# One-hot rows of 16 tokens in four instructions, and matches of ranks in half precision, in a two-block transformer kernel

## The chip, the core and the metric

The kernel runs on one NeuronCore of a Trainium2 chip. The metric is the device time of one execution in microseconds (us), the median over several executions.

## The reference, cut to what matters

The reference is two blocks, one behind the other, over 512 tokens of width 1024. The first block is attention and retention, then a layer of 16384 single-neuron experts whose choice is a product of keys:

```python
s = einsum('thpd,hpkd->thpk', q, subkeys)        # 8 heads, 2 halves, 128 keys
s_top, i_top = top_k(s, 16)                      # the 16 best keys of each half
cand = s_top[:, :, 0, :, None] + s_top[:, :, 1, None, :]
c_top, c_idx = top_k(cand, 16)                   # the 16 best of 256 pairs
i1 = take_along_axis(i_top[:, :, 0], c_idx // 16)
i2 = take_along_axis(i_top[:, :, 1], c_idx % 16)
g = softmax(c_top)                               # gates of expert i1 * 128 + i2
out = sum over the 128 chosen of g * gelu(u[e] . x) * v[e]
```

The second block (attention with chosen keys, a pooling branch, gates) follows it and is not touched here.

## The kernel before, in words

Four tiles of 128 tokens. For three of them the kernel doesn't gather the chosen experts but computes all of them: `hidden_tensor` multiplies the tokens with every expert row (128 **expert steps** of 128 experts, called j in the code), and `combine_tensor` multiplies the gated result with every value row. The gates are needed as a dense table for this, gate[expert, token], mostly zero. The fourth tile gathers its rows with indirect transfers in the combine stage.

**The hidden stage** (`hidden_sync`, `hidden_tensor`, `hidden_scalar`, `hidden_vector`, from L1371). In an expert step ACT rounds the loaded `u_raw` to `u_high` (L1424) as soon as TensorE has freed one of three buffers, VectorE makes `u_low`, the rest of it (L1453), TensorE does 24 matmuls of 512 columns (L1402), ACT evicts the sum with Gelu (L1440), and SP stores it. `u_high` and `u_low` are made two steps ahead: both wait for the end of the step before the present one.

**The background.** The choice of experts and the table of gates are made inside the same stage. Each engine has a generator for them, and takes `pace(j)` pieces of it in step j (L937), after its split of step j + 2 on VectorE and ACT; TensorE takes each piece in four parts, spread between its 24 matmuls, behind the matmuls 1, 4, 7 and so on where two pieces fall into a step. A piece has the same number on every engine; the order of the pieces and the pace are written by hand. The engines are coupled by semaphores, so a piece that is late on VectorE stops TensorE where it asks for it.

**The choice** (`choose_vector`, L1193). For each tile: eight pieces find the 16 best keys of two halves each, four pieces the 16 best pairs of two heads each, one computes the gate. Then the ranks are matched: the chosen pair number is cut in two digits, and for each half the digit is compared with all 16 ranks (`is_equal`, L1237), multiplied with the key numbers head by head (L1243, eight instructions) and summed (L1246). The last sum releases `picked`; in the piece behind it TensorE transposes keys and gates (L1153), and ACT moves them to `chosen`. There are 19 pieces a tile, and TensorE asks for `picked` in piece 19.

**The gates** (`gates_vector`, `gates_tensor`, `gates_scalar`, L1282). One piece of header, then 24 blocks of 16 tokens in 4 pieces each. VectorE makes for each token a row `hot1` (key number equal to key1) and two rows `weighed` (equal to key2, times the rounded gate and its rest), 128 elements each: 12 instructions and 4 tokens a piece (L1349, L1351), each piece releasing `hot_parts` once. TensorE multiplies `hot1` and `weighed` of a token in two matmuls of 128 columns (L1294), ACT moves them to a stage (L1316), and six stages of 4 MB are stored from ACT's queue. VectorE makes block n + 1 while TensorE multiplies block n, and there are two buffers of each.

Of the kernel before, what the change touches and what calls it, by code (L numbers as in the profile page):

```python
# [4 lines left out]
F32 = mybir.dt.float32  # L5
F32R = mybir.dt.float32r
F16 = mybir.dt.float16
I32 = mybir.dt.int32
U32 = mybir.dt.uint32
ALU = mybir.AluOpType  # L10
ACT = mybir.ActivationFunctionType
AX_X = mybir.AxisListType.X

P = 128
# [12 lines left out]
PEER_HEADS, PEER_TOPK, N_KEYS = 8, 16, 128  # L27
HK = PEER_HEADS * PEER_TOPK
HP = PEER_HEADS * 2
# [883 lines left out]
TD = DENSE * P  # L913
GATE_CHUNK = 64
CHUNKS = TD // GATE_CHUNK
HOT = 16
BLOCKS = TD // HOT
COMBINE_BANKS = (4, 5, 6, 7, 0, 1)
HALF_TILES = [(half, t) for half in range(2) for t in range(TT)]
# [3 lines left out]
GATE_SCALE = 2.0 ** 15  # L923
BATCH = 4
# [7 lines left out]
CHOICE_STEPS = HP // 2 + PEER_HEADS // 2  # L932
# [2 lines left out]


def pace(j):  # L937
    return 1 + (j % 4 == 3) if j < 64 else 2


def tile_of(i):
# [9 lines left out]
class Peer:  # L951
    def __init__(self, m, keep):
        nc = m.nc
        region = Region(nc, keep.rows_at)
# [13 lines left out]
        region = Region(nc, after_scores)  # L968
# [1 line left out]
        self.cand = [region.tensor(f"candidates{i}", [P, PEER_TOPK, PEER_TOPK], F32) for i in range(2)]  # L970
        self.top = region.tensor("top", [P, HP, PEER_TOPK], F32)
        self.places = region.tensor("places", [P, HP, PEER_TOPK], U32)
        self.keys = region.tensor("top_keys", [P, HP, PEER_TOPK], F32)
        self.best = region.tensor("best", [P, PEER_HEADS, PEER_TOPK], F32)
        self.best_at = region.tensor("best_at", [P, PEER_HEADS, PEER_TOPK], U32)
        self.digit = region.tensor("digit", [P, 2, PEER_HEADS, PEER_TOPK], U32)
        self.digit_value = region.tensor("digit_value", [P, 2, PEER_HEADS, PEER_TOPK], F32)
        self.match = region.tensor("match", [P, PEER_HEADS * PEER_TOPK, PEER_TOPK], F32)
        self.picked = region.tensor("picked", [P, 3, HK], F32)
        self.total = region.tensor("gate_total", [P, 2, PEER_HEADS], F32)  # L980

        region = Region(nc, self.scores_at)
        self.stages = [region.tensor(f"gate_stage{i}", [P, N_KEYS, GATE_CHUNK], F32) for i in range(2)]
        self.every_key = region.tensor("every_key", [P, N_KEYS], F16)
        self.rounded = region.tensor("gate_rounded", [P, TD], F16)
        self.key_values = [region.tensor(f"key_value{i}", [P, TD], F32) for i in range(2)]
        self.parts = [region.tensor(f"gate_part{i}", [P, TD], F32) for i in range(2)]
        self.hot1 = [region.tensor(f"hot1_{i}", [P, HOT, N_KEYS], F16) for i in range(2)]
        self.weighed = [[region.tensor(f"hot2_part{p}_{i}", [P, HOT, N_KEYS], F16) for p in range(2)] for i in range(2)]

        at_raw, at_pairs = Region(nc, self.u_raw_at), Region(nc, keep.stream_at)
        self.u_raw = [at_raw.tensor(f"u_raw{i}", [P, KT, P], F32) for i in range(U_RAW)]
# [6 lines left out]
        region = Region(nc, self.scores_at)  # L999
# [142 lines left out]
def choose_tensor(m, keep, p):  # L1142
    pe, s = m.pe, m.s
    yield
    for t in range(TT):
        for _ in range(CHOICE_STEPS + 6):
            yield
        if t < DENSE:
            b = GATE_BANKS[t % 4]
            pe.wait_ge(s.picked, t + 1)  # L1150
            m.await_bank(b)
            for i in range(3):
                step = pe.engine.transpose(m.bank[b][:, i * P:i * P + P], p.picked[:, i, :], keep.ident[:, :])  # L1153
            step.then_inc(s.picked_turned, 1)
            m.bank_freed[b] = (s.picked_moved, 3 * t + 3)
        yield


def choose_scalar(m, keep, p):
    act, s = m.act, m.s  # L1160
    yield
    for t in range(TT):
        for _ in range(CHOICE_STEPS):
            yield
        act.wait_ge(s.gate_shifted, t + 1)
        act.engine.activation(p.picked[:, 2, :], p.picked[:, 2, :], ACT.Exp).then_inc(s.gate_powered, 1)
        for _ in range(6):
            yield
        if t < DENSE:
            b = GATE_BANKS[t % 4]  # L1170
            act.wait_ge(s.picked_turned, t + 1)
            for i in range(3):
                act.engine.activation(p.chosen[i][:, t * P:t * P + P], m.bank[b][:, i * P:i * P + P], ACT.Copy).then_inc(s.picked_moved, 1)
        yield
# [18 lines left out]
def choose_vector(m, keep, p):  # L1193
    dve, s = m.dve, m.s
    v = dve.engine
# [3 lines left out]
    for t in range(TT):  # L1199
# [3 lines left out]
                              for i in range(2)])  # L1203
            yield
        dve.settle()
        dve.step(v.tensor_copy(p.keys[:, :, :], p.places[:, :, :]))
        for h in range(0, PEER_HEADS, 2):
            for i in range(2):
                a = p.top[:, 2 * (h + i), :].unsqueeze(2).broadcast_to([P, PEER_TOPK, PEER_TOPK])
# [6 lines left out]
        gate = p.picked[:, 2, :].rearrange("p (h k) -> p h k", h=PEER_HEADS)  # L1216
        wide = [P, PEER_HEADS, PEER_TOPK]
# [11 lines left out]
        dve.settle()  # L1229
        dve.step(v.tensor_tensor(gate, gate, p.total[:, 1, :].unsqueeze(2).broadcast_to(wide), ALU.mult))  # L1230
        yield
        for half in range(2):
            wide = [P, HK, PEER_TOPK]
            ranks = keep.counting[:, 0:PEER_TOPK].unsqueeze(1).broadcast_to(wide)
            chosen_rank = p.digit_value[:, half, :, :].rearrange("p h k -> p (h k)").unsqueeze(2).broadcast_to(wide)
            dve.settle()
            dve.step(v.tensor_tensor(p.match[:, :, :], chosen_rank, ranks, ALU.is_equal))  # L1237
            dve.settle()
            yield
            for h in range(PEER_HEADS):  # L1240
                part = p.match[:, h * PEER_TOPK:(h + 1) * PEER_TOPK, :]
                of_rank = p.keys[:, 2 * h + half, :].unsqueeze(1).broadcast_to([P, PEER_TOPK, PEER_TOPK])
                dve.step(v.tensor_tensor(part, part, of_rank, ALU.mult))  # L1243
            dve.settle()
            yield
            found = v.tensor_reduce(p.picked[:, half, :], p.match[:, :, :], AX_X, ALU.add)  # L1246
            if half == 0:
                dve.step(found)
            else:
                found.then_inc(s.picked, 1)  # L1250
        yield
        if t == DENSE:
            place_rows(m, keep, p)
# [28 lines left out]
def gates_tensor(m, keep, p):  # L1282
    pe, s = m.pe, m.s
    for _ in range((1 + 4 + 3) * BATCH):
        yield
    for n in range(BLOCKS):
        for q in range(HOT // BATCH):
            b = GATE_BANKS[q % 4]
            pe.wait_ge(s.hot_parts, 4 * n + q + 1)
            m.await_bank(b)  # L1290
            for i in range(BATCH):
                for part in range(2):
                    t = q * BATCH + i
                    step = pe.engine.matmul(m.bank[b][:, i * P:i * P + P], p.hot1[n % 2][:, t, :], p.weighed[n % 2][part][:, t, :],  # L1294
                                            start=(part == 0), stop=(part == 1))
                if i == BATCH - 1:
                    step.then_inc(s.gates_built, 1)
                    m.bank_freed[b] = (s.gates_moved, 4 * n + q + 1)
                yield


def gates_scalar(m, keep, p):
# [6 lines left out]
    for n in range(BLOCKS):  # L1309
        for q in range(HOT // BATCH):  # L1310
            at = n * HOT + q * BATCH
# [13 lines left out]
def gates_vector(m, keep, p):  # L1325
    dve, s = m.dve, m.s
    v = dve.engine
    gate = p.chosen[2]
    key1, key2 = p.key_values
    dve.wait_ge(s.picked_moved, 3 * DENSE)  # L1330
    dve.step(v.tensor_copy(p.every_key[:, :], keep.counting[:, :]))
    for i in range(2):
        dve.step(v.tensor_copy(p.key_values[i][:, :], p.chosen[i][:, :]))
    dve.step(v.tensor_scalar(p.rounded[:, :], gate[:, :], GATE_SCALE, None, ALU.mult))
    dve.settle()
    dve.step(v.tensor_copy(p.parts[0][:, :], p.rounded[:, :]))
    dve.step(v.scalar_tensor_tensor(out=p.parts[1][:, :], in0=gate[:, :], scalar=GATE_SCALE, in1=p.rounded[:, :],
                                    op0=ALU.mult, op1=ALU.subtract))
    dve.settle()
    yield  # L1340

    def make_hot(n):
        if n >= 2:
            dve.wait_ge(s.gates_built, 4 * (n - 1))
        for q in range(HOT // BATCH):
            for i in range(BATCH):
                t = q * BATCH + i
                token = slice(n * HOT + t, n * HOT + t + 1)
                v.tensor_scalar(p.hot1[n % 2][:, t, :], p.every_key[:, :], key1[:, token], None, ALU.is_equal)  # L1349
                for half in range(2):  # L1350
                    step = v.tensor_scalar(p.weighed[n % 2][half][:, t, :], p.every_key[:, :], key2[:, token],  # L1351
                                           p.parts[half][:, token], ALU.is_equal, ALU.mult)
            step.then_inc(s.hot_parts, 1)
            yield

    yield from make_hot(0)
    for _ in range(3):
        yield
    for n in range(BLOCKS):
        following = make_hot(n + 1) if n + 1 < BLOCKS else iter(())  # L1360
        for q in range(HOT // BATCH):
            next(following, None)
            yield
        for _ in following:
            yield
# [1367 lines left out]
```

## Time and profile before

| what | value |
|---|---|
| median of 3 runs | 2216.58 us (2207.34 to 2219.11) |
| the profiled execution | 2214.67 us |
| its span | 2213.4 us |
| TensorE busy | 2076.5 us, 94% |
| VectorE busy | 1450.8 us, 66% |
| ScalarE (ACT) busy | 760.6 us, 34% |
| GpSimd (POOL) busy | 362.3 us, 16% |
| granted TensorE clock, mean | 0.977 |

A profile is one execution. Busy times are the union of an engine's instructions; weight loads of TensorE (PEld) are counted apart and overlap its matmuls. Matmuls overlap each other in the records, so the distance of two starts says what one costs, not its duration. A wait stands in brackets in the timeline, with the instruction that ended it.

### The profile page before, as it was taken

The numbers are of one execution on the slowest core, as the hardware profiler recorded it, in microseconds if no ns is written. First come the engines' busy times: TensorE is split into PE (matmuls) and PEld (weight loads), VectorE is DVE, ScalarE is ACT, GpSimd is POOL, SyncE is SP. The second block draws the span as 40 slices with busy tenths as digits, with TensorE's granted clock in tenths as the row PEclk, the third lists the DMA queues.
The fourth block names the chain that finished last, engine by engine and source line by source line (L and its number), as shares of the span: only waits on it lengthen the run. The fifth ranks groups of instructions, "written<-read, shape, count | busy, mean of one in ns | idle before, by whom it ended". The sixth has DMA issues, their size and how long they took to land.

```text
span 2213.4 us, 25835 instructions
## 1 busy us (share of the span) xinstructions
PE 2076.5 (94%) x9641; PEld 1626.2 (73%) x9641; DVE 1450.8 (66%) x3415; ACT 760.6 (34%) x1101; POOL 362.3 (16%) x262
## 2 busy tenths in 40 slices
PE   6989999999999999999999998998889969999899
PEld 5767778878787866666677886777768757777677
DVE  4465432587787988888823576777678854876434
ACT  4334431332332333333333332222222354334531
POOL 0000000000000000000002647677675200000000
PEclk9999999999999999999999999999999979999999
DMA  5221132234443435555575879888889812221022
GB/s 165 84 57 57 58 105 95 96 129 145 132 149 130 143 115 190 191 190 191 187 284 188 284 284 332 316 331 327 318 317 375 293 37 67 77 77 58 20 96 86
DMA packets 148077, 374.90 MB, mean 169 GB/s; under 512 B 19440, under 2 KB 60912, under 8 KB 138736
## 3 DMA queue, kind: packets, MB, share of 16 engines
q1 hardware_dynamic: 121536, 277.03, 37.0%
q0 software_dynamic: 22528, 67.19, 8.1%
q10 hardware_dynamic: 3888, 29.03, 3.3%
q8 instruction: 76, 1.25, 0.2%
q14 instruction: 49, 0.40, 0.1%
HBM read 312.38 MB, written 60.82 MB: 169 GB/s over the span
## 4 chain that ended last, share of the span: by engine, by line
PE 61%; DVE 15%; DMA 7%; ACT 6%; issue 6%; POOL 6%; SPq 1%; ACTq 0%; DVEq 0%
PE bank L1402 27%; PE bank L305 9%; PE bank L306 9%; PE bank L307 9%; POOL row_unit L1542 5%; DMA v_raw<-in_peer_v 5%; PE bank L1294 2%; DVE x L1662 2%; DVE v_low L1651 1%; DMA row<-in_peer_v,row_places 1%; DVE u_low L1453 1%; DVE hidden_in L1640 1%; ACT v_high L1601 1%; PE bank L1954 1%; POOL row L1535 1%
## 5 line engine op out<-in xcount | busy, mean ns | idle before, releaser
L1402 PE MATMUL bank<-xn_low,u_high 128*128 128x512 f32 x1024 | 433.7, 424 | 0.0
L1402 PE MATMUL bank<-xn_high,u_high 128*128 128x512 f32 x1024 | 403.3, 394 | 0.0
L1402 PE MATMUL bank<-xn_high,u_low 128*128 128x512 f32 x1024 | 402.5, 393 | 0.0
L1535 POOL DMA_INDIRECT row<-in_peer_v,row_places x128 | 189.4, 1480 | 1278.6 <-DMA gates_scratch<-gate_stage 1135.3
L305 PE MATMUL bank<-v_high,w_high 128*128 128x512 f32 x768 | 309.7, 403 | 54.0 <-DVE v_low L1651 54.0
L306 PE MATMUL bank<-v_low,w_high 128*128 128x512 f32 x768 | 307.1, 400 | 0.0
L307 PE MATMUL bank<-v_high,w_low 128*128 128x512 f32 x768 | 306.1, 399 | 0.0
L298 DVE TENSOR_TENSOR weights_low<-weights_raw,weights_high 128x1024 fp32r<-128x1024 f32 (+1 forms) x105 | 127.3, 1217 | 232.0 <-ACT weights_high L289 231.8
L1453 DVE TENSOR_TENSOR u_low<-u_raw,u_high 128x1024 fp32r<-128x1024 f32 x128 | 156.4, 1222 | 174.5 <-ACT u_high L1424 174.1
L1402 PEld LDWEIGHTS bank<-xn_high,u_high 128*128 128x128 f32 x1024 | 193.3, 189 | 41.2
L305 PEld LDWEIGHTS bank<-v_high,w_high 128*128 128x128 f32 x768 | 148.9, 194 | 94.3 <-DVE v_low L1651 63.0
L1402 PEld LDWEIGHTS bank<-xn_high,u_low 128*128 128x128 f32 x1024 | 194.8, 190 | 25.2
L1402 PEld LDWEIGHTS bank<-xn_low,u_high 128*128 128x128 f32 x1024 | 194.2, 190 | 25.3
L1351 DVE TENSOR_SCALAR hot_part<-every_key,key_value,gate_part 128x128 f16<-128x128 f16 x768 | 203.3, 306 | 0.0
L1601 ACT ACTIVATE v_high<-v_raw 128x2048 fp32r<-128x2048 f32 x64 | 122.2, 1911 | 220.7 <-DMA v_raw<-in_peer_v 119.5
L1662 DVE SCALAR_TENSOR_TENSOR x<-row,row_weight,x 128x1024 f32<-128x1024 f32 x128 | 164.1, 1282 | 46.5 <-DMA row<-in_peer_v,row_places 30.5
L1651 DVE TENSOR_TENSOR v_low<-v_raw,v_high 128x2048 fp32r<-128x2048 f32 x64 | 146.3, 2287 | 68.6 <-ACT v_high L1601 68.4
L1542 POOL DMA_INDIRECT row_unit<-hidden_scratch,unit_places x128 | 169.1, 1321 | 97.1 <-DMA hidden_scratch<-hidden 58.4
L307 PEld LDWEIGHTS bank<-v_high,w_low 128*128 128x128 f32 x768 | 149.0, 194 | 32.4
L306 PEld LDWEIGHTS bank<-v_low,w_high 128*128 128x128 f32 x768 | 149.0, 194 | 30.8
L1440 ACT ACTIVATE hidden<-bank 128x512 f32<-128x512 f32 x128 | 76.5, 598 | 276.4 <-PE bank L1402 272.5
L289 ACT ACTIVATE weights_high<-weights_raw 128x1024 fp32r<-128x1024 f32 (+1 forms) x105 | 109.8, 1051 | 173.4 <-PE bank L307 171.1
(334 smaller groups left out, 3255.4 us busy)
## 6 DMA issues: line engine op xcount, KB each, us to landing
u_raw<-in_peer_u SPq DMA_DIRECT2D x128, 512.0 KB, 3.7
v_raw<-in_peer_v SPq DMA_DIRECT2D x64, 1024.0 KB, 7.7
weights_raw<-in_w_in SPq DMA_DIRECT2D x64, 512.0 KB, 3.6
hidden_scratch<-hidden SPq DMA_DIRECT2D x128, 256.0 KB, 2.2
gates_scratch<-gate_stage ACTq DMA_DIRECT2D x6, 4096.0 KB, 13.2
gate_in<-gates_scratch SPq DMA_DIRECT2D x192, 128.0 KB, 6.6
hidden_in<-hidden_scratch SPq DMA_DIRECT2D x32, 768.0 KB, 9.7
weights_raw<-in_w_out SPq DMA_DIRECT2D x16, 512.0 KB, 3.6
```

The lines of the kernel that those rows point to most:

```text
L298: dve.engine.tensor_tensor(st.part(st.low[n % st.PAIRS], n), st.part(st.raw[n % st.RAW], n), st.part(st.high[n % st.PAIRS], n).bitcast(F32 ...
L305: engine.matmul(out, lh, rh, start=first, stop=False)
L306: engine.matmul(out, lh, rl, start=False, stop=False)
L307: return engine.matmul(out, ll, rh, start=False, stop=last)
L1351: step = v.tensor_scalar(p.weighed[n % 2][half][:, t, :], p.every_key[:, :], key2[:, token], p.parts[half][:, token], ALU.is_equal, ALU.mult)
L1402: step = pe.engine.matmul(m.bank[b][:, :], left[:, k, :], right[:, k, :], start=(done == 0), stop=(done == 3 * KT - 1))
L1453: dve.engine.tensor_tensor(p.u_low[j % U_PAIRS][:, :, :], p.u_raw[j % U_RAW][:, :, :], p.u_high[j % U_PAIRS][:, :, :].bitcast(F32), ALU.su ...
L1535: pool.engine.indirect_dma_start(p.row[i % ROWS][:, :], None, values, bass.IndirectOffsetOnAxis(p.row_places[:, i:i + 1], 0)).then_inc(s.r ...
L1542: pool.engine.indirect_dma_start(p.unit[:, i:i + 1], None, units, bass.IndirectOffsetOnAxis(p.unit_places[:, i:i + 1], 0)).then_inc(s.unit ...
L1601: act.engine.activation(p.v_pair[n % 2][0][:, :, :], p.v_raw[n % 2][:, :, :], ACT.Copy).then_inc(s.v_high, 1)
L1651: v.tensor_tensor(low[:, :, :], p.v_raw[n % 2][:, :, :], high[:, :, :].bitcast(F32), ALU.subtract).then_inc(s.v_low, 1)
L1662: v.scalar_tensor_tensor(out=keep.x[:, 0, :], in0=p.row[i % ROWS][:, :], scalar=p.row_weight[:, i:i + 1], in1=keep.x[:, 0, :], op0=ALU.mul ...
```

## The change

The rows of 16 tokens are made by four instructions in place of 48. For this, rows of two tokens are laid in turn, so that a row of tensors has the shape 8 x 128 x 2, and TensorE reads each token's row with a pitch of two elements. The second key's rows go to a buffer of their own, `hot2`, and are multiplied with the two parts of the gate. TensorE waits for both parts of a whole block. Match, ranks, key numbers and parts of gates become 16-bit; the match takes both halves in one `is_equal` and is summed by halving in place of a reduction. The choice has 18 pieces a tile, and the pace is raised from five pieces in four steps to three in two, up to step 52 in place of 64.

```diff
-    return 1 + (j % 4 == 3) if j < 64 else 2
+    return 1 + j % 2 if j < 52 else 2
@@ Peer: tensors
-        self.keys = region.tensor("top_keys", [P, HP, PEER_TOPK], F32)
+        self.keys = region.tensor("top_keys", [P, PEER_HEADS, 2, PEER_TOPK], F16)
-        self.digit_value = region.tensor("digit_value", [P, 2, PEER_HEADS, PEER_TOPK], F32)
-        self.match = region.tensor("match", [P, PEER_HEADS * PEER_TOPK, PEER_TOPK], F32)
+        self.digit_value = region.tensor("digit_value", [P, 2, PEER_HEADS, PEER_TOPK], F16)
+        self.ranks = region.tensor("ranks", [P, PEER_TOPK], F16)
+        self.match = region.tensor("match", [P, 2, HK, PEER_TOPK], F16)
...
+        self.every_key = region.tensor("every_key", [P, N_KEYS, TWO], F16)
+        self.parts = [region.tensor(f"gate_part{i}", [P, TD], F16) for i in range(2)]
+        rows = [P, HOT // TWO, N_KEYS, TWO]
+        self.hot1 = [region.tensor(f"hot1_{i}", rows, F16) for i in range(2)]
+        self.hot2 = region.tensor("hot2", rows, F16)
+        self.weighed = [[region.tensor(f"hot2_part{p}_{i}", rows, F16) for p in range(2)] for i in range(2)]
@@ choose_tensor, choose_scalar
-        for _ in range(CHOICE_STEPS + 6):
+        for _ in range(CHOICE_STEPS + 5):
...
-        for _ in range(6):
+        for _ in range(5):
@@ choose_vector
+        wide = [P, 2 * HK, PEER_TOPK]
+        match = p.match[:, :, :, :].rearrange("p a k r -> p (a k) r")
+        if t == 0:
+            dve.step(v.tensor_copy(p.ranks[:, :], keep.counting[:, 0:PEER_TOPK]))
+            dve.settle()
+        chosen_rank = p.digit_value[:, :, :, :].rearrange("p a h k -> p (a h k)").unsqueeze(2).broadcast_to(wide)
+        dve.step(v.tensor_tensor(match, chosen_rank, p.ranks[:, :].unsqueeze(1).broadcast_to(wide), ALU.is_equal))
+        dve.settle()
+        yield
         for half in range(2):
...
+            part = p.match[:, half, :, :].rearrange("p (h k) r -> p h k r", h=PEER_HEADS)
+            of_rank = p.keys[:, :, half, :].unsqueeze(2).broadcast_to([P, PEER_HEADS, PEER_TOPK, PEER_TOPK])
+            dve.step(v.tensor_tensor(part, part, of_rank, ALU.mult))
+        dve.settle()
+        yield
+        n = PEER_TOPK // 2
+        while n > 1:
+            dve.step(v.tensor_tensor(match[:, :, 0:n], match[:, :, 0:n], match[:, :, n:2 * n], ALU.add))
+            dve.settle()
+            n //= 2
+        yield
+        both = p.picked[:, 0:2, :].rearrange("p a k -> p (a k)")
+        v.tensor_tensor(both, match[:, :, 0], match[:, :, 1], ALU.add).then_inc(s.picked, 1)
         yield
@@ gates_tensor
-            pe.wait_ge(s.hot_parts, 4 * n + q + 1)
+            pe.wait_ge(s.hot_parts, 2 * n + 2)
...
+                    t, of_two = divmod(q * BATCH + i, TWO)
+                    step = pe.engine.matmul(m.bank[b][:, i * P:i * P + P], p.hot1[n % 2][:, t, :, of_two],
+                                            p.weighed[n % 2][part][:, t, :, of_two], start=(part == 0), stop=(part == 1))
@@ gates_vector
-    for i in range(2):
-        dve.step(v.tensor_copy(p.key_values[i][:, :], p.chosen[i][:, :]))
...
+    def by_token(row, n):
+        return row[:, n * HOT:(n + 1) * HOT].rearrange("p (t a) -> p t a", a=TWO).unsqueeze(2).broadcast_to(shape)
...
+        dve.step(v.tensor_tensor(p.hot1[n % 2][:, :, :, :], every, by_token(key1, n), ALU.is_equal))
+        yield
+        dve.wait_ge(s.hot_parts, 2 * n)
+        dve.step(v.tensor_tensor(p.hot2[:, :, :, :], every, by_token(key2, n), ALU.is_equal))
+        dve.settle()
+        yield
+        for half in range(2):
+            v.tensor_tensor(p.weighed[n % 2][half][:, :, :, :], p.hot2[:, :, :, :], by_token(p.parts[half], n),
+                            ALU.mult).then_inc(s.hot_parts, 1)
             yield
```

`make_hot(n)` still waits, for n of 2 and more, until TensorE has built block n - 2 (`gates_built` at 4 (n - 1)).

## Rows read from the trace of the kernel before

**Rows 1.** Part 1 of the page: busy us (share of the span), instructions.

```profile
PE 2076.5 (94%) x9641; PEld 1626.2 (73%) x9641; DVE 1450.8 (66%) x3415; ACT 760.6 (34%) x1101; POOL 362.3 (16%) x262
```

**Rows 2.** Table by windows of 100 us; columns: PE, PEld, DVE, ACT, POOL busy, PEclk, DMA share, GB/s.

```profile
900.00:1000.00 100.00, 100.00 (x570) 63.98 (x570) 86.16 (x351) 37.90 (x57) 0.00 (x0) 1.00 0.51 182
...
1100.00:1200.00 100.00, 100.00 (x470) 78.92 (x469) 31.70 (x53) 31.99 (x40) 5.12 (x4) 1.00 0.59 211
```

**Rows 3.** The chain that ended last, a stretch of the hidden stage: start us, us.

```profile
405.35 38.11 PE bank L1402 x168
```

**Rows 4.** Waits, 400 to 770 us, engine PE: us in total, times, longest.

```profile
PE bank L1153 <- DVE picked L1246: 9.5, 3, 3.5
```

**Rows 5.** Timeline of ACT and PE around the second wait for `picked`.

```profile
535.23 0.60 ACT L1440 ACTIVATE hidden<-bank 128x512 f32<-128x512 f32 x1 [3.89 <-PE bank L1402]
...
578.55 0.39 PE L1402 MATMUL bank<-xn_high,u_high 128*128 128x512 f32 x1
...
582.41 0.90 PE L1153 MATMUL bank<-ident,picked 128*128 128x128 f32 x3 [3.47 <-DVE picked L1246]
...
582.96 0.78 PE L1402 MATMUL bank<-xn_low,u_high 128*128 128x512 f32 x1
...
584.82 0.60 PE L1402 MATMUL bank<-xn_high,u_low 128*128 128x512 f32 x1
...
585.24 0.40 PE L1402 MATMUL bank<-xn_high,u_high 128*128 128x512 f32 x1
```

**Rows 6.** Timeline of VectorE: start us, us, instruction, count, idle before in brackets.

```profile
423.31 1.23 DVE L1453 TENSOR_TENSOR u_low<-u_raw,u_high 128x1024 fp32r<-128x1024 f32 x1 [1.87 <-ACT u_high L1424]
...
429.13 1.21 DVE L1453 TENSOR_TENSOR u_low<-u_raw,u_high 128x1024 fp32r<-128x1024 f32 x1
...
471.28 0.28 DVE L1220 TENSOR_TENSOR picked<-best 128x128 f32<-128x128 f32 x1
...
472.95 2.29 DVE L1237 TENSOR_TENSOR match<-digit_value,counting_sb 128x2048 f32<-128x2048 f32 x1
...
536.81 1.23 DVE L1453 TENSOR_TENSOR u_low<-u_raw,u_high 128x1024 fp32r<-128x1024 f32 x1 [1.87 <-ACT u_high L1424]
...
547.10 1.21 DVE L1453 TENSOR_TENSOR u_low<-u_raw,u_high 128x1024 fp32r<-128x1024 f32 x1
...
552.70 1.20 DVE L1453 TENSOR_TENSOR u_low<-u_raw,u_high 128x1024 fp32r<-128x1024 f32 x1
...
566.41 2.77 DVE L1243 TENSOR_TENSOR match<-match,top_keys 128x256 f32<-128x256 f32 x8
...
580.08 2.28 DVE L1246 TENSOR_REDUCE picked<-match 128x128 f32<-128x2048 f32 x1
```

**Rows 7.** Timeline of PE and DVE in one expert step with gates.

```profile
905.93 0.40 PE L1402 MATMUL bank<-xn_high,u_high 128*128 128x512 f32 x1
...
907.71 1.23 DVE L1453 TENSOR_TENSOR u_low<-u_raw,u_high 128x1024 fp32r<-128x1024 f32 x1 [0.94 <-ACT u_high L1424]
...
908.86 0.25 DVE L1349 TENSOR_SCALAR hot<-every_key,key_value 128x128 f16<-128x128 f16 x1
...
909.69 0.28 PE L1294 MATMUL bank<-hot_part,hot 128*128 128x128 f16 x2
```

**Rows 8.** Groups of instructions, shapes apart: busy us, mean ns, idle before.

```profile
L1294 PEld LDWEIGHTS bank<-hot_part,hot 128*128 128x128 f16 x768 | 44.5, 98 | 106.4 <-issue 106.4
...
L1402 PEld LDWEIGHTS bank<-xn_high,u_high 128*128 128x128 f32 x1024 | 193.3, 189 | 41.2
...
L2321 DVE TENSOR_TENSOR normed_two<-x,final_gain 128x512 f32<-128x512 f32 x8 | 5.4, 690 | 0.2
...
L1243 DVE TENSOR_TENSOR match<-match,top_keys 128x256 f32<-128x256 f32 x64 | 22.1, 417 | 0.1
```

**Rows 9.** Timeline of VectorE, the header of the gates.

```profile
762.32 0.36 DVE L1336 CAST gate_part<-gate_rounded 128x384 f32<-128x384 f16 x1
...
762.60 0.55 DVE L1337 SCALAR_TENSOR_TENSOR gate_part<-gate,gate_rounded 128x384 f32<-128x384 f32 x1
```

More of the change, by code:

```diff
@@ L916 @@
 HOT = 16
+TWO = 2
 BLOCKS = TD // HOT
@@ L983, in __init__ @@
         self.stages = [region.tensor(f"gate_stage{i}", [P, N_KEYS, GATE_CHUNK], F32) for i in range(2)]
[L984 to L989, printed above, removed]
+        self.every_key = region.tensor("every_key", [P, N_KEYS, TWO], F16)
[4 more added lines that the diff above has]
+        self.weighed = [[region.tensor(f"hot2_part{p}_{i}", rows, F16) for p in range(2)] for i in range(2)]
         at_raw, at_pairs = Region(nc, self.u_raw_at), Region(nc, keep.stream_at)
@@ L1205, in choose_vector @@
         dve.settle()
-        dve.step(v.tensor_copy(p.keys[:, :, :], p.places[:, :, :]))
+        dve.step(v.tensor_copy(p.keys[:, :, :, :].rearrange("p h a r -> p (h a) r"), p.places[:, :, :]))
         for h in range(0, PEER_HEADS, 2):
@@ L1231, in choose_vector @@
         yield
-        for half in range(2):
-            wide = [P, HK, PEER_TOPK]
-            ranks = keep.counting[:, 0:PEER_TOPK].unsqueeze(1).broadcast_to(wide)
-            chosen_rank = p.digit_value[:, half, :, :].rearrange("p h k -> p (h k)").unsqueeze(2).broadcast_to(wide)
-            dve.settle()
[L1237 to L1250, printed above, removed]
+        wide = [P, 2 * HK, PEER_TOPK]
[7 more added lines that the diff above has]
+        yield
+        for half in range(2):
+            part = p.match[:, half, :, :].rearrange("p (h k) r -> p h k r", h=PEER_HEADS)
[6 more added lines that the diff above has]
+            dve.step(v.tensor_tensor(match[:, :, 0:n], match[:, :, 0:n], match[:, :, n:2 * n], ALU.add))
+            dve.settle()
+            n //= 2
+        yield
+        both = p.picked[:, 0:2, :].rearrange("p a k -> p (a k)")
+        v.tensor_tensor(both, match[:, :, 0], match[:, :, 1], ALU.add).then_inc(s.picked, 1)
         yield
@@ L1292, in gates_tensor @@
                 for part in range(2):
-                    t = q * BATCH + i
-                    step = pe.engine.matmul(m.bank[b][:, i * P:i * P + P], p.hot1[n % 2][:, t, :], p.weighed[n % 2][part][:, t, :],
-                                            start=(part == 0), stop=(part == 1))
+                    t, of_two = divmod(q * BATCH + i, TWO)
+                    step = pe.engine.matmul(m.bank[b][:, i * P:i * P + P], p.hot1[n % 2][:, t, :, of_two],
+                                            p.weighed[n % 2][part][:, t, :, of_two], start=(part == 0), stop=(part == 1))
                 if i == BATCH - 1:
@@ L1327, in gates_vector @@
     v = dve.engine
-    gate = p.chosen[2]
-    key1, key2 = p.key_values
+    key1, key2, gate = p.chosen
+    shape = [P, HOT // TWO, N_KEYS, TWO]
+    every = p.every_key[:, :, :].unsqueeze(1).broadcast_to(shape)
     dve.wait_ge(s.picked_moved, 3 * DENSE)
-    dve.step(v.tensor_copy(p.every_key[:, :], keep.counting[:, :]))
-    for i in range(2):
-        dve.step(v.tensor_copy(p.key_values[i][:, :], p.chosen[i][:, :]))
-    dve.step(v.tensor_scalar(p.rounded[:, :], gate[:, :], GATE_SCALE, None, ALU.mult))
+    dve.step(v.tensor_copy(p.every_key[:, :, :], keep.counting[:, :].unsqueeze(2).broadcast_to([P, N_KEYS, TWO])))
+    dve.step(v.tensor_scalar(p.parts[0][:, :], gate[:, :], GATE_SCALE, None, ALU.mult))
     dve.settle()
-    dve.step(v.tensor_copy(p.parts[0][:, :], p.rounded[:, :]))
-    dve.step(v.scalar_tensor_tensor(out=p.parts[1][:, :], in0=gate[:, :], scalar=GATE_SCALE, in1=p.rounded[:, :],
+    dve.step(v.scalar_tensor_tensor(out=p.parts[1][:, :], in0=gate[:, :], scalar=GATE_SCALE, in1=p.parts[0][:, :],
                                     op0=ALU.mult, op1=ALU.subtract))
@@ L1344, in make_hot @@
             dve.wait_ge(s.gates_built, 4 * (n - 1))
[L1345 to L1353, printed above, removed]
+        dve.step(v.tensor_tensor(p.hot1[n % 2][:, :, :, :], every, by_token(key1, n), ALU.is_equal))
[7 more added lines that the diff above has]
+                            ALU.mult).then_inc(s.hot_parts, 1)
             yield
```

## The prediction

> **What bounds the kernel now.** I read the page's shares first: TensorE is busy for 94% of the span, VectorE for 66% [rows 1]. The change touches only work that runs in the background of the hidden stage (the 128 expert steps of `hidden_tensor`, from 405 us to 1198 us), so the table by stage came next. Between 900 and 1200 us TensorE is busy all the time at a granted clock of 1.00, while VectorE is at 86% as long as gate rows are built and at 32% after them [rows 2]. The hidden stage is therefore TensorE's: 24 matmuls of 512 columns a step, which the chain shows at 38.11 us for 168, or 0.227 us each and 5.44 us a step [rows 3]. VectorE's work costs time there only where TensorE waits for it. The list of waits has one such entry in this stage: the transposes of the chosen keys wait three times for the last match of ranks, 9.5 us together [rows 4]. One row of it, in order of time: TensorE issues its last matmul at 578.55 and gets its transposes at 582.41; after them five starts take 585.24 - 582.96 = 2.28 us in place of 5 x 0.227, a fall of the clock that costs 1.15 us more [rows 5]. So all that a faster VectorE can give is about 9.5 + 3 x 1.15 = 13 us. Faster rows of gates give nothing by themselves, since TensorE doesn't wait for them now.
>
> **The matches of ranks.** What counts is VectorE's stretch between its last idle moment in a tile and the end of the match, against the time at which TensorE comes to its transposes.
> Before: VectorE starts `u_low` at 536.81, after an idle time, and ends the match at 580.08 + 2.28 = 582.36 [rows 6]; that is the wait of 3.5 us.
> After, the code gives 18 background steps a tile in place of 19, and three in two expert steps in place of five in four, so a tile takes exactly 12 expert steps. Counted from its start, expert step +5 holds score pieces 7 and 8, +6 candidate piece 1, +7 pieces 2 and 3, +8 piece 4, +9 the gate and `is_equal`, +10 the products, +11 the sums; TensorE asks at +12, after one matmul. VectorE's times, all with a `u_low`, from [rows 6]: +5: 429.13 - 423.31 = 5.82. A candidate piece with `u_low` is 552.70 - 547.10 = 5.60, so 4.45 without (`u_low` holds the engine for 1.15, by 907.71 to 908.86 in [rows 7]). +6: the stretch 536.81 to 547.10 had the cast and two pieces, 10.29, less 4.45 = 5.84. +7: 5.60 + 4.45 = 10.05. +8: 5.60. +9: 1.13, the gate 472.95 - 471.28 = 1.67, and `is_equal` over 4096 elements. +10: 1.15 and two products of 2048. +11: 1.15 and sums of 2048, 1024, 512 and 256.
> The prices of these half precision operations are in no row. From above, they run like the f32 ones: 2.29 us for 2048 elements [rows 6], 1.23 for 1024, 0.69 for 512, 0.417 for 256 [rows 8]. From below, twice as fast again as half of that: 0.69 for 2048. VectorE has a double rate: 384 elements with one source take 0.36 us, with two f32 sources 0.55 [rows 9]. The operands that run in neighbouring 16-bit pairs carry two elements in the bytes of one f32, so I take the time of half as many elements: 1.23, 0.69, 0.42 for products and the first sums. `is_equal` reads one rank 16 times over, as its f32 form does, and the last sum reads every sixteenth element; I take them at the f32 rate: 2.29 + 2 x 1.06 = 4.41 and 0.42.
> The Trainium skill (Vector Engine (DVE) Microarchitecture Reference, 5.1 Performance modes) says that a two-source operation that reads one 2-byte element 16 times runs at single rate; by this rule `is_equal` gains nothing from half precision, and were it not so, it would take 2.29 us and the waits would grow by nothing. No run here shows it yet.
> +9 is 7.24, +10 3.56, +11 1.15 + 2.88 = 4.03. Sum: 5.82 + 5.84 + 10.05 + 5.60 + 7.24 + 3.56 + 4.03 = 42.1 us. A step's start is where ACT begins the eviction, 535.23, and `u_low` begins 1.58 us later [rows 5, 6]; TensorE asks at 7 x 5.44 - 1.58 + 0.23 = 36.7 us. So it waits 5.4 us in place of 3.5, though the match itself shrank from two rounds of 2.29 + 2.77 + 2.28 [rows 6] to 9.7 us: the faster pace brings TensorE to the question earlier by more than the match got shorter. Three tiles: **+6 us**. The clock falls after each wait already; with a longer gap I add 0.7 us each, **+2 us** (between 0 and 4). The expert matmuls themselves don't wait: `u_low` ends 1.58 + 1.23 us into a step and is used two steps of 5.44 on, 8 us later, more than the lag of 5.4.
>
> **The rows of gates.** Removed are 48 instructions of 128 elements for 16 tokens; added are 4 of 2048. 16 tokens take two expert steps, of 7.04 us each by my sum of 24 x 0.227 and 16 gate matmuls at 0.1 us (a 98 ns load each [rows 8]). VectorE has two `u_low` and four rows of 1.23 us in 14.1 us: it falls from 86% to about 50%. That is beside TensorE's work and brings nothing.
> But the order changes. Before, TensorE's first batch of a block waited for a quarter of the block that was made a whole block earlier. Now it waits for 2n + 2 parts, the second weighed part of the block. By the pace and the count of steps (choice 73, header 8, so the first block is background step 81, in expert step 53) this part is made in the first background step of an expert step, and TensorE needs it in the second one of the same expert step. The place of both is in the trace: TensorE starts an expert step at 905.93 and issues its fifth pair at 909.69; VectorE starts `u_low` at 907.71 and its next instruction at 908.86 [rows 7]. VectorE can't be earlier, for `u_low` waits for ACT's `u_high`, and that for a buffer that TensorE frees with the step before. With 1.23 us the part is ready at 910.09, plus 0.05 for the signal: TensorE waits 0.45 us, at each of 23 blocks: **+10 us**. Bounds: nothing at 0.69 us (909.55), 1.5 x 23 = 35 us at 2.29.
>
> **The matmuls of gates** read rows and weights with a pitch of two elements. Weights of f16 load in 98 ns [rows 8]. No row has a pitch; from below it costs nothing, from above it is like the f32 load, which covers the same bytes in 189 ns: 768 x 91 ns = 70 us. I take nothing, since 128 columns are taken one by one in both, and a load of 98 ns has the length of the f32 one's half.
> The Trainium skill (TensorE: Matmul & The Clock Gate, Weight-path perf modes) has 16-bit weights read two at a time in the fast mode, which a pitch might spoil, though it lists strided reads among those allowed.
>
> **What moves.** The gates end some 13 expert steps earlier, 71 us less the 18 of above. The six 4 MB stores on ACT's queue go with them and still overlap loads of 512 KB, at a DMA share of 0.5 [rows 2]. The last one no longer meets the first loads of the combine stage; TensorE didn't wait there, so nothing. VectorE's header of casts (one background step) and the cast to `ranks` are under 1 us and lie in slack.
>
> **Sum**: 6 + 2 + 10 = 18 us on the profiled execution of 2214.67 us (span 2213.4): 2232.7. That execution is 1.9 us under the median of 2216.58, so the forecast for a median is **2234 us**, 0.8% slower. I count 0.5%, 11 us, as what a measurement can tell from no change.
>
> **Rivals.**
> (a) The half precision operations get no double rate (the row of a pair is repeated, which no row shows). Then the gate part costs 35 us and the products and sums 4.0 us more per tile, 12 in all: 2216.6 + 8 + 35 = 2260, with the match 2272. For it: every two-source row here is at the single rate. Chance 0.12.
> (b) The pitch of two slows the weight loads: 70 us, which in turn covers the waits for the parts (TensorE comes later): 2216.6 + 8 + 70 = 2295. Chance 0.08.
> (c) The waits stay as they are, because half precision is faster than I take it (`is_equal` at 2.29 us, or the weighed part under 0.83 us, which is 909.69 - 908.86). Then 0 to 10 us remain: 2216 to 2226. Chance 0.16.
> (d) Faster: the three waits for the match vanish with their clock falls, -13 us: 2203. Place: step +12 of each tile. It decides at 36.7 us of VectorE work, 5.4 less than my sum; `is_equal` at 2.29 gives 2.1, products and sums at twice the speed again some 2.3, and a transfer that gains from stores that end earlier would have to do the rest. Chance 0.08.
> The forecast's own case has 0.56; its spread, 2224 to 2242, has a small part below the 11 us. So: slower 0.68, same 0.24, faster 0.08. The range 2212 to 2262 holds (c), the forecast and (a) without its worst; out are (b), most of (d) and the end of (a).
>
> **What would show it.** Right: waits of TensorE for the last sum of the match of 5 to 6 us, three times; a new wait of the gate matmuls for the weighed rows, 23 times at 0.4 to 0.5 us; `is_equal` at 4.4 us, hot rows at 1.2 us; gate weight loads at 98 ns; VectorE at about 50% from 750 to 1050 us; the hidden stage 18 us longer and the combine stage as long as before. Wrong: no wait at the first batch of a block, a match wait under 3.5 us, or a combine stage that changed its length by more than 5 us.

## The result, and the profile after

The changed kernel takes 2229.3 us (median of 9 runs) against 2211.71 us for the kernel before in runs on the same chips: a ratio of 1.008, interval 1.0055 to 1.0105. That is 0.8% slower, as forecast; the forecast of 2234 us stood on a median of before of 2216.58.

The waits of TensorE in the hidden stage (engine, line, what it waited for: us in total, times, longest), on its matmul queue:

```profile
PE bank L1156 <- DVE picked L1258: 17.4, 3, 5.9
PE bank L1302 <- DVE hot_part L1361: 6.6, 23, 0.3
```

and on its weight loads:

```profile
PEld bank L1156 <- DVE picked L1258: 18.6, 3, 6.3
PEld bank L1302 <- DVE hot_part L1361: 16.5, 23, 0.7
```

The first line of each answers to [rows 4]: the three waits for the match grew from 9.5 to 17.4 us. The second is new: 23 short waits for the rows of gates. The table by stage, columns as in [rows 2]:

```profile
500.00:600.00 100.00, 94.29 (x406) 77.59 (x405) 85.99 (x343) 29.67 (x40) 0.00 (x0) 0.97 0.39 131
900.00:1000.00 100.00, 97.99 (x554) 62.03 (x553) 49.47 (x42) 37.33 (x56) 0.00 (x0) 1.00 0.51 184
```

VectorE is at 49% in the stage of the gates, where it was at 86% [rows 2], and TensorE, which had no gap there, has lost 2%. VectorE's groups, by form (busy us, mean ns, idle before):

```profile
L1361 DVE TENSOR_TENSOR hot_part<-hot,gate_part 128x2048 f16<-128x2048 f16 x48 | 58.5, 1221 | 0.8
L1354 DVE TENSOR_TENSOR hot<-every_key,key 128x2048 f16<-128x2048 f16 x24 | 29.2, 1218 | 0.0
L1241 DVE TENSOR_TENSOR match<-digit_value,ranks 128x4096 f16<-128x4096 f16 x4 | 17.7, 4420 | 0.0
L1247 DVE TENSOR_TENSOR match<-match,top_keys 128x2048 f16<-128x2048 f16 x8 | 9.4, 1218 | 0.0
L1302 PEld LDWEIGHTS bank<-hot_part,hot 128*128 128x128 f16 x768 | 44.2, 98 | 115.4 <-issue 98.9 <-DVE hot_part L1361 16.5
```

2048 elements in neighbouring pairs take 1.22 us, `is_equal` over 4096 takes 4.42, and weights with a pitch of two elements load in 98 ns as those without [rows 8].

**Where the match's wait is.** The timeline around the second tile's match, VectorE then TensorE (start us, us; idle before in brackets):

```profile
509.17 1.23 DVE L1462 TENSOR_TENSOR u_low<-u_raw,u_high 128x1024 fp32r<-128x1024 f32 x1 [1.50 <-ACT u_high L1433]
...
539.14 4.42 DVE L1241 TENSOR_TENSOR match<-digit_value,ranks 128x4096 f16<-128x4096 f16 x1
...
544.74 2.35 DVE L1247 TENSOR_TENSOR match<-match,top_keys 128x2048 f16<-128x2048 f16 x2
...
548.27 2.59 DVE L1253 TENSOR_TENSOR match<-match 128x2048 f16<-128x2048 f16 x3
...
550.90 0.62 DVE L1258 TENSOR_TENSOR picked<-match 128x256 f32<-128x256 f16 x1
```

```profile
545.47 0.39 PE L1411 MATMUL bank<-xn_high,u_high 128*128 128x512 f32 x1
551.57 0.90 PE L1156 MATMUL bank<-ident,picked 128*128 128x128 f32 x3 [5.71 <-DVE picked L1258]
552.12 0.78 PE L1411 MATMUL bank<-xn_low,u_high 128*128 128x512 f32 x1
...
556.96 0.56 PE L1411 MATMUL bank<-xn_high,u_high 128*128 128x512 f32 x1
557.36 0.40 PE L1411 MATMUL bank<-xn_low,u_high 128*128 128x512 f32 x1
```

VectorE works without a pause from 509.17 to 551.52, 42.35 us (forecast 42.1); TensorE is free for its question 0.23 us after 545.47, so 36.5 us into it (forecast 36.7). After the wait twelve starts take 557.36 - 552.12 = 5.24 us in place of 12 x 0.227: the low clock costs 2.5 us here, where it cost 1.15 in [rows 5]. This is the most costly of the three tiles, though. After the third wait, of the same 5.7 us, it lasts for six starts and costs 1.3 us:

```profile
626.40 0.78 PE L1411 MATMUL bank<-xn_low,u_high 128*128 128x512 f32 x1
...
629.05 0.39 PE L1411 MATMUL bank<-xn_low,u_high 128*128 128x512 f32 x1
```

Read off the starts in the same way, the three tiles have 8, 12 and 6 slow starts (1.7, 2.5 and 1.3 us, 5.5 together) after waits of 5.9, 5.7 and 5.7 us, and in the kernel before 8, 5 and 7 (1.5, 1.1 and 1.4 us, 4.1 together) after waits of 2.5, 3.5 and 3.5 us. So the clock costs 1.4 us more in all, and the length of the wait alone doesn't say for how long it stays low.

**Where the match's wait was before.** The prediction takes VectorE's stretch before from 536.81, but that isn't its last idle moment. It stood idle once more, in the step of the first `is_equal`:

```profile
559.74 0.31 ACT L1166 ACTIVATE picked<-picked 128x128 f32<-128x128 f32 x1 [5.34 <-DVE picked L1220]
...
561.37 0.60 ACT L1440 ACTIVATE hidden<-bank 128x512 f32<-128x512 f32 x1
...
562.95 1.23 DVE L1453 TENSOR_TENSOR u_low<-u_raw,u_high 128x1024 fp32r<-128x1024 f32 x1 [1.87 <-ACT u_high L1424]
```

ACT, in its piece of the exponent, waited 5.34 us for VectorE's late gate; the eviction and `u_high` behind it came late, and VectorE waited 1.87 us for them. The second and third tile of the kernel before both have this, so some 1.9 of their 3.5 us came round by way of ACT (an estimate from these rows; no run takes it away alone). In the change ACT waits as long (5.70 us), but VectorE spends that time in its one long `is_equal` and doesn't stand idle.

**Where the wait for the rows is.** One block in the stage of the gates:

```profile
880.33 1.22 DVE L1462 TENSOR_TENSOR u_low<-u_raw,u_high 128x1024 fp32r<-128x1024 f32 x1 [3.42 <-ACT u_high L1433]
881.47 1.22 DVE L1361 TENSOR_TENSOR hot_part<-hot,gate_part 128x2048 f16<-128x2048 f16 x1
```

```profile
882.07 0.39 PE L1411 MATMUL bank<-xn_high,u_high 128*128 128x512 f32 x1
882.74 0.29 PE L1302 MATMUL bank<-hot_part,hot 128*128 128x128 f16 x2 [0.29 <-DVE hot_part L1361]
```

The part ends at 882.69, and the pair, which follows its matmul by 0.24 us elsewhere, follows it by 0.67. The list of the matmul queue puts 0.29 us on this wait, because the records of matmuls overlap; what it costs is in the distance of starts. `u_low` of this step starts at 880.33 and the one two steps on at 894.86, 14.53 us, where a step took 7.04 before (907.71 [rows 7], and 900.67 for the `u_low` ahead of it), so 14.08 for two: 0.45 us a block.

### The profile page after: what moved, and what is told of

Same layout as the page of the kernel before. It is cut to its first block, busy times and chain, and to the rows that moved or that the text cites. A ratio compares the mean times of both kernels' runs of the same rounds, so it can differ in the third digit from the quotient of the medians.

```text
span 2219.6 us, 24648 instructions
## 1 busy us (share of the span) xinstructions
PE 2074.3 (93%) x9641; PEld 1624.5 (73%) x9641; DVE 1308.1 (59%) x2305; ACT 760.8 (34%) x1101; POOL 358.2 (16%) x262
## 3 DMA queue, kind: packets, MB, share of 16 engines
q1 hardware_dynamic: 121536, 277.03, 36.7%
## 4 chain that ended last, share of the span: by engine, by line
PE 60%; DVE 18%; ACT 7%; issue 7%; DMA 5%; POOL 3%; SPq 0%; ACTq 0%; DVEq 0%
PE bank L1411 24%; PE bank L305 10%; PE bank L306 9%; PE bank L307 9%; DMA v_raw<-in_peer_v 4%; DVE x L1671 3%; POOL row_unit L1551 3%; DVE u_low L1462 2%; PE bank L1302 2%; DVE v_low L1660 2%; DVE hot_part L1361 1%; ACT u_high L1433 1%; DVE hidden_in L1649 1%; ACT v_high L1610 1%; ACT w_high L1616 1%
## 5 line engine op out<-in xcount | busy, mean ns | idle before, releaser
L305 PE MATMUL bank<-h_high,weights_high 128*128 128x512 f32 (+1 forms) x328 | 136.6, 416 | 5.9 <-DVE ret_q L774 2.5
```

What stands on the lines that cost most here:

```text
L305: engine.matmul(out, lh, rh, start=first, stop=False)
```

## The stage lengths, by kernel

Since TensorE bounds the hidden stage, I measure it by itself: from the first expert matmul that reads `xn_low` to the first matmul of the combine stage. The line of each that answers it, before and after (ns min/median/max, first and last start):

```profile
L1402 PE MATMUL bank<-xn_low,u_high x1024: 387/389/775, 405.4 to 1193.6; 128*128 128x512 f32 x171
L305 PE MATMUL bank<-v_high,w_high x768: 387/389/796, 1194.1 to 1795.9; 128*128 128x512 f32 x192
```

```profile
L1411 PE MATMUL bank<-xn_low,u_high x1024: 387/389/776, 406.7 to 1214.7; 128*128 128x512 f32 x171
L305 PE MATMUL bank<-v_high,w_high x768: 387/389/796, 1215.2 to 1803.4; 128*128 128x512 f32 x192
```

Before: 1194.1 - 405.4 = 788.7 us; after: 808.5. The combine stage (from one first start to the last of the second line) takes 601.8 and 588.2. The same for every kernel run (one execution each; before and the change were profiled twice):

| kernel | hidden, us | waits for the match / for rows (matmul queue), us | combine, us | ratio to before (95%) |
|---|---|---|---|---|
| before | 788.7 | 9.5 / 0 | 601.8 | 1 |
| the change | 808.5 | 17.4 / 6.6 | 588.2 | 1.008 (1.0055 to 1.0105) |
| e1 pace alone | 809.4 | 26.0 / 0 | 597.5 | 1.0083 (1.0069 to 1.0098) |
| e2 match alone | 797.9 | 17.4 / 0 | 604.7 | 1.0037 (1.0024 to 1.0051) |
| e3 gates alone | 799.9 | 9.5 / 6.6 | 599.8 | 1.0038 (1.0025 to 1.0051) |
| e4 one more piece | 798.9 | 17.4 / 0 | 589.8 | 1.0036 (1.0023 to 1.0048) |
| e5 old pace | 791.0 | 5.0 / 6.6 | 600.9 | 1.0009 (0.9991 to 1.0028) |
| e6 ask later | 784.3 | 0 / 6.6 | 598.6 | 0.9972 (0.9954 to 0.999) |
| e7 both | 774.0 | 0 / 0 | 593.8 | 0.9928 (0.9903 to 0.9953) |
| e8 before, ask later | 774.1 | 0 / 0 | 601.6 | 0.9941 (0.9918 to 0.9963) |
| e9 rows of one | 832.5 | 17.4 / 30.9 | 600.5 | 1.0176 (1.0143 to 1.0209) |
| e10 before again | 788.1 | 9.5 / 0 | 603.7 | one run |
| e11 the change again | 808.6 | 17.4 / 6.6 | 594.9 | one run |
| e12 rows of one, both | 779.9 | 0 / 0 | 598.7 | 0.9951 (0.9935 to 0.9966) |

## The experiments

**e1, the pace alone.** The kernel before with one line:

```diff
-    return 1 + (j % 4 == 3) if j < 64 else 2
+    return 1 + j % 2 if j < 52 else 2
```

> The kernel before with nothing but the new pace (three pieces in two expert steps up to step 52). Theory (TensorE's question comes by the pace, VectorE's answer by the length of the match): the old match takes 14.7 us where the new one takes 9.7, in a tile of 12.7 expert steps in place of 15.2, so the three waits for the match become 26 to 27 us together (before 9.5), and the whole hidden stage, 789 us before, becomes 806 to 812; the kernel 0.8% to 1.1% slower than before. Rival (the waits come from the new match itself, for example from its chain of small dependent sums): the three waits stay near 9.5 us and the time is the same as before.

26.0 us of waits and a hidden stage of 809.4 us, as expected:

```profile
PE bank L1153 <- DVE picked L1246: 26.0, 3, 10.2
```

So the wait comes from the pace. The shorter match, with the one piece less that it takes in a tile, gets 26.0 - 17.4 = 8.6 us of it back; e5 below shows that it is a gain at the old pace too.

**e2, match and pace with the old rows of gates** (`gates_vector`, `gates_tensor` and their tensors as before).

> The new match in half precision with its 18 pieces and the new pace; rows and matmuls of gates as before. Theory: the waits for the match are 17 to 18 us as in the changed kernel, no gate matmul waits for its rows; hidden stage 8 to 11 us longer than before (797 to 800 us), the kernel about 0.4% slower. Rival (the rows of gates carry all of the loss): same as before within 3 us.

797.9 us, +9.2, and the same 17.4 us of waits. Of the 9.2, the list has 7.9; the other 1.3 is the clock (slow starts that cost 5.4 us in the three tiles against 4.1 before).

**e3, the rows of gates alone** (the rest as before).

> Only the rows of 16 tokens in four instructions, with the wait for both parts; match and pace as before. Theory: 23 waits of about 0.45 us and nothing else, hidden stage 10 us longer than before (798 to 800), VectorE under 55% busy in the stage of the gates, the kernel about 0.45% slower. Rival (the match carries all of the loss, the short waits are hidden by the queue of TensorE): hidden stage as before, 789.

799.9 us, +11.2. The two halves add up: 9.2 + 11.2 = 20.4, and the whole change has 19.8.

**e4, one more empty piece** between header and first block, in the generators of TensorE, ACT and VectorE:

```diff
-    for _ in range((1 + 4 + 3) * BATCH):
+    for _ in range((1 + 4 + 4) * BATCH):
...
-    for _ in range(1 + 4 + 3):
+    for _ in range(1 + 4 + 4):
...
-    for _ in range(3):
+    for _ in range(4):
```

> The changed kernel with one more empty piece between header and first block on all three engines, so that the second weighed part is made in the second piece of an expert step and asked for in the first piece of the next. Theory: the 23 waits of the gate matmuls for their rows vanish, those for the match stay at 17 to 18 us; hidden stage 10 us shorter than in the changed kernel (808.8), so 797 to 800; the kernel 0.4% slower than before. Rival (the matmuls themselves are slower with a pitch of two, the waits are only where it shows): the stage stays over 805.

798.9 us: the short waits are gone, the stage is 9.6 us shorter than in the change, and VectorE's work is the same. It is within 1.0 us of e2, whose rows have no pitch, so the pitch costs no more than that.

**e5, the change with the pace of before.**

> The changed kernel with the pace of before. Theory: a tile of 18 pieces takes 14.4 expert steps, VectorE's match is shorter than before, so the three waits for it fall under those of before (9.5 us) to about 5 us together; the 23 waits of the gates stay, 10 us; hidden stage 4 to 7 us longer than before (793 to 796). Rival (the pace changes nothing): 808, as the changed kernel.

791.0 us, +2.3, where I had expected 4 to 7. The wait was as expected, in two tiles only:

```profile
PE bank L1156 <- DVE picked L1258: 5.0, 2, 3.0
```

I had left out that shorter waits also give clock back: the granted clock between 400 and 800 us is 1.00 here and 0.99 before. By the starts, five slow ones follow the wait of 3.0 us, and none the other, of 2.0 us.

This run sets the match apart. It differs from e3 only in the match, at the old pace, and its stage is 799.9 - 791.0 = 8.9 us shorter; at the new pace e2 is 11.5 us shorter than e1. The pace costs 20.7 us with the old match (e1) and 808.5 - 791.0 = 17.5 with the new one. So the new match is a gain at either pace, and the +9.2 of match and pace together is the difference of the two. This is shown in the stage; in the total the intervals of e3 and e5 overlap a little.

**e6, the question for the match three pieces later,** in TensorE's and ACT's generators (the exponent stays in its piece):

```diff
+ASKED = 3
...
-        for _ in range(CHOICE_STEPS + 5):
+    for tile in range(TT):
+        for piece in range(CHOICE_STEPS + 5 + 1):
+            if tile and piece == ASKED:
+                t = tile - 1
...
             yield
-        if t < DENSE:
```

> The changed kernel with the transposes and moves of the chosen keys asked for three pieces later, in the fourth piece of the next tile. Theory: no wait for the match, no fall of the clock, the 23 waits of the gates stay: hidden stage 787 to 791, about 18 to 20 us shorter than in the changed kernel and level with before. Rival (VectorE's lag then shows as late u_low instead): the stage stays over 800 with waits of the expert matmuls for u_low.

784.3 us, 3 us under the range. The stage is 24.2 us shorter than in the change: 17.4 of waits, and 6.8 that I put down to the clock, where I had allowed for 1 to 3. No `u_low` was late.

**e7, both repairs.**

> The changed kernel with both: the question for the match three pieces later and one more empty piece before the blocks. Theory: TensorE never waits in the background, hidden stage 777 to 780 us against 789 before; the kernel 0.4% to 0.6% faster than before. Rival (what is won in the hidden stage is lost again in the combine stage): same as before in the total though the stage is shorter.

774.0 us, 3 us under the range again, and the kernel is 0.7% faster than before. TensorE has no gap in the stage:

```profile
500.00:600.00 100.00, 100.00 (x444) 82.74 (x444) 94.14 (x352) 33.44 (x45) 0.00 (x0) 1.00 0.41 136
900.00:1000.00 100.00, 100.00 (x568) 63.95 (x567) 48.96 (x42) 39.00 (x59) 0.00 (x0) 1.00 0.53 191
```

**e8, the kernel before with the later question only.**

> The kernel before, with its match in f32, its rows of single tokens and its pace, and only the question for the match three pieces later. Theory (nothing of the change is needed, only TensorE's waits count): no waits for the match, hidden stage 777 to 780 us, the same as with all of the change and both repairs. Rival (half precision is needed for it): waits remain and the stage is over 783.

774.1 us, also 3 us under its range. The ranges of e6 to e8 held too little for the clock. Against before the stage gives 14.6 us, of which the list has 9.5, so what goes with the waits, the clock above all, is 5.1 us and not 3 x 1.15. With f32 matches and rows of single tokens the stage is as short as with all of the change and both repairs. The intervals of e7 and e8 overlap; which is faster is not shown.

**e9, rows of one token after the other.**

```diff
-TWO = 2
+TWO = 1
```

> The changed kernel with the rows of one token after the other (the constant for two tokens set to one), so that the token's key is one element read 128 times and TensorE reads without a pitch. Theory: the four instructions of a block lose the double rate and take 2.29 us each in place of 1.22; the second weighed part is ready 1.5 us after TensorE's question in place of 0.45; hidden stage 808.5 + 24 = 832 to 835 us, the kernel 1.8% to 2.0% slower than before; gate weight loads stay at 98 ns. Rival (the order of the rows does not matter for the rate): 1.22 us each, stage as in the changed kernel.

The rate falls by half, and the stage becomes 24.0 us longer than in the change, 1.04 a block, as expected:

```profile
L1361 DVE TENSOR_TENSOR hot_part<-hot,gate_part x48: 2283/2286/2292, 711.4 to 1078.3; 128x2048 f16<-128x2048 f16 x48
L1302 PEld LDWEIGHTS bank<-hot_part,hot x768: 95/97/101, 722.2 to 1093.8; 128*128 128x128 f16 x192
```

With the 11.2 us of e3 the gates then cost 35.2 us, the 35 of the prediction's rival (a): it would have held for rows that aren't laid in pairs.

**e10 and e11, before and the change once more.**

> The kernel before once more, for the length of its stages in a second execution. Theory (the combine stage varies by execution, through its transfers, and not by kernel): hidden stage 788 to 790 us as in the first profile, combine stage anywhere from 588 to 605 where the first had 601.8. Rival (it is a property of the kernel): combine stage within 2 us of 601.8.

> The changed kernel once more. Theory: hidden stage 808 to 809 us again, combine stage anywhere from 588 to 605 where the first profile had 588.2. Rival (stores of gates that end 50 us earlier make the combine stage shorter): combine stage within 2 us of 588.2.

The hidden stages repeat within 0.6 us (788.1, 808.6). The combine stage of the change was 594.9 us after 588.2, so the second execution rules out a fixed length; that of before (603.7 after 601.8) fits both readings.

**e12, both repairs with rows of one.**

> Both repairs (question for the match three pieces later, one more empty piece) with rows of one token after the other, at 2.29 us an instruction. Theory (VectorE's rate in the gates does not count as soon as TensorE asks a piece later): hidden stage 774 us, the same as with the interleaved rows, although VectorE works some 24 blocks x 4.2 = 100 us more. Rival (VectorE becomes late by itself): waits for rows or u_low, stage over 778.

779.9 us, not 774: a miss. The table's matmul queue shows no wait, but the weight loads do:

```profile
PEld bank L1302 <- DVE hot_part L1361: 12.2, 23, 0.5
```

With the extra piece both weighed parts fall into one expert step, and the next step asks for them with its first pair. At 2.29 us each they are late:

```profile
883.44 4.49 DVE L1361 TENSOR_TENSOR hot_part<-hot,gate_part 128x2048 f16<-128x2048 f16 x2
```

```profile
887.49 0.40 PE L1411 MATMUL bank<-xn_high,u_high 128*128 128x512 f32 x1
887.98 0.28 PE L1302 MATMUL bank<-hot_part,hot 128*128 128x128 f16 x2
```

The pair follows its matmul by 0.49 us in place of 0.24, 0.25 too late, and 23 x 0.25 = 5.8 is the difference found. A move by one piece gives slack for 1.22 us instructions and not quite for 2.29.

## Why the prediction was right, point by point

- **The bound.** Right: 143 us less of VectorE time in the profile (1308.1 against 1450.8 us busy) brought nothing, and where TensorE's waits were taken away (e7, e8) the stage fell to 774 us, 14.6 less than before; I had counted 13, with too little for the clock.
- **The matches of ranks, +6 us and +2 for the clock.** Right in place, and near in size: +9.2 in e2, of which the waits are 7.9. The terms of the last two sums were too small: those of 512 and 256 elements took 0.64 and 0.62 us in place of 0.42 each, so step +11 took 4.40 us in place of 4.03, and the other steps were 0.16 shorter together. (The recorded terms of that step add to 3.91 and not 4.03; by them the wait is 5.3.) The waits were 5.7 to 5.9 us by the list in place of 5.4. The kernel before was read wrongly in two places: its first wait was 2.5 us and not 3.5, so that 5.4 in each tile means 6.7 us more and not 6, and its stretch held the idle time shown above. Neither entered the 42.1 us for the change, where VectorE has no such idle time. The clock's 0.7 us more a tile was 0.5 on the mean of three, and between equal waits it goes from 1.3 to 2.5, so that this term came near is partly luck.
- **The cause.** e1 shows what the prediction argued from counts of steps: the pace brings the question too early. The match is innocent: it takes 8.9 us off the stage at the old pace (e3, e5) and 11.5 at the new one (e1, e2).
- **The rows of gates, +10 us.** Right: 0.45 us at each of 23 blocks, 11.2 us in e3 and 9.6 in e4.
- **The pitch, nothing.** Right: 98 ns, and 97 in e9 without it.
- **What moves, nothing.** Not settled. Six 4 MB stores end 50 us earlier, before and after:

```profile
POOL row L1535 <- DMA gates_scratch<-gate_stage: 1135.3, 1, 1135.3
```

```profile
POOL row L1544 <- DMA gates_scratch<-gate_stage: 1085.4, 1, 1085.4
```

  The prediction's own sign of being wrong, a combine stage that changes by more than 5 us, was met: it was 13.6 us shorter in the first pair of profiles and 8.8 (594.9 against 603.7) in the second. The combine stages of kernels with early stores lie between 588 and 605 us and those with late ones between 600 and 604; the profiled execution of the change was 13.6 us shorter there than that of before, which is why its span, 2219.6 us, is only 6.2 us longer while the medians differ by 17.6. Over the medians the loss in total (17.6) is 2 us under the loss in the hidden stage (19.8), which is inside the interval. A gain of some us in the combine stage from the earlier stores is neither shown nor ruled out.
- **Rivals.** (a) needs rows without pairs (e9); (b) was refuted by the weight loads, and by e4; (d) needed VectorE's answer within 36.7 us and (c) within 40, or a weighed part under 0.83 us; they came at 42.35 and took 1.22.

## What to carry to other kernels

Where the bounding engine runs through a fixed order of background pieces, ask of every edit when the bounding engine will ask and when the other will answer, in steps of the loop; the helper's busy share (86% to 49% here) says nothing about it. A piece that is released only when it is whole should be asked for in a later loop step than the one in which its last part is made. Judge each part of a change at a fixed pace: the new match by itself is a gain, and only together with the new pace a loss. Before rewriting the helper's arithmetic, move the question: three pieces of delay in the old kernel (e8) gave 0.6% and a hidden stage as short as any measured.

## What the runs showed of the hardware that I had not expected

- Short rows cost: the sum over 512 half precision elements in rows of 2 with a pitch of 16 elements took 636 ns, nearly as long as that over 1024 in rows of 4, 701 ns, while 2048 in rows of 8 took 1218; and 256 single elements took 628.

```profile
L1253 DVE TENSOR_TENSOR match<-match 128x2048 f16<-128x2048 f16 x4 | 4.9, 1218 | 0.0
L1253 DVE TENSOR_TENSOR match<-match 128x1024 f16<-128x1024 f16 x4 | 2.8, 701 | 0.1
L1253 DVE TENSOR_TENSOR match<-match 128x512 f16<-128x512 f16 x4 | 2.5, 636 | 0.1
L1258 DVE TENSOR_TENSOR picked<-match 128x256 f32<-128x256 f16 x4 | 2.5, 628 | 0.1
```

  The Trainium skill (Vector Engine (DVE) Microarchitecture Reference, 5.2 Measured stream behaviour on trn2) says, of streams of 4-byte elements, that a port keeps its full rate only for runs of at least two neighbouring 4-byte words; rows of two 2-byte elements are runs of one word, rows of four are runs of two, and these rows agree with it. The interleaved keys, though, read one word of two elements 128 times over, and kept the double rate at 1218 ns.
- The time that the clock stays low after a wait isn't given by the wait: 8, 12 and 6 slow starts after waits of 5.9, 5.7 and 5.7 us, 8, 5 and 7 after 2.5, 3.5 and 3.5, five after 3.0 and none after 2.0 (e5).
